# Expert token lists written by indirect transfers in place of one-hot products

## Chip, cores and metric

The kernel runs on one core of one Trainium2 chip. The metric is the device time of one launch in microseconds. Lower is better.

## What is computed

A sequence of 2048 tokens plus 16 meta tokens (2064 in all), 1024 wide, goes through one layer: a pooling mixer, then a mixture of 16 experts in which each expert chooses its tokens, then a last normalisation. The part that matters here, cut from the reference:

```python
cap = CAPACITY_FACTOR * T // N_EXPERTS           # 258
aff = jax.nn.softmax(u @ router_w, axis=-1)
g, idx = lax.top_k(jnp.swapaxes(aff, 1, 2), cap) # per expert: gate and token of each slot
xs = u[idx]                                      # 258 rows of 1024
hid = silu(xs @ w_gate) * (xs @ w_up)            # 2048 wide
ys = (hid @ w_down) * g[..., None]
out = zeros.at[idx].add(ys)
```

A "list" below is the 258 token numbers and gates of one expert.

## The kernel before

**Stages.** The pooling mixer runs over 19 overlapping tiles of 128 tokens (NT = 19). Then comes the routing: affinities, a threshold search over 10 rounds that finds each expert's 258th value, and prefix sums (TensorE) from which `find_slots` works out for each of the 19 x 128 token places and each expert the slot that the token takes in the expert's list, or a slot far off if it isn't chosen. Then a loop over 15 experts (`Fori(0, NE - 1)` on every engine), and expert 15 by itself with the last normalisation beside it.

**One expert.** Products are in fp32 made of two rounded parts: `w_hi` (ScalarE, line 734), `w_lo` (VectorE, line 1061, `split_rest`), and three products for each pair of blocks (`products`, line 1167), 258 columns wide. The work is cut into 48 "quarters" of 24 matmuls, QE = 48: 32 for gate and up (four rounds b of eight, `gate_up`), 16 for down (`down_quarter`). Weights arrive on SP's queue in pieces of 1 MiB into four buffers (`raw`), two quarters a piece, and the splits run up to three quarters ahead of TensorE. `silu` on ScalarE, `hid` and `hid_lo` on VectorE (lines 1090, 1096) stand between the up quarters and the down ones.

**The list of the next expert.** It is made inside the loop for expert n + 1 while expert n runs. On VectorE, after quarter 3 of each round, `pick(n + 1, 5 * b)` compares `iota` with the slot of five token tiles: five one-hot tiles `picks` of 128 x 272 (line 1038), 20 in four rounds. On TensorE, between the last up quarter and the first down quarter, `make_list(n + 1, n + 1)` multiplies the 19 one-hot tiles with `vals` (token number in two digits, affinity in three bf16 parts), 3 x 19 = 57 matmuls. On VectorE, after the split in down quarter 0 and the three copies of the old list (`idx_now`, `gates_now`, `idx_small`, lines 1115 to 1117), `read_list(n + 1)` turns the sums into `idx`, `idx_chunk` and `gates` in six small steps (lines 1044 to 1056). GpSimd waits for them, then starts the three gathers of rows of `u_rows` (`gather`, lines 532, 535), and after the expert's end three accumulating scatters into `h_acc` (lines 578, 580). TensorE turns the gathered rows after down quarter 7 (`turn_pair`).

**Order.** Each engine runs its own list of instructions in order, and semaphores tie them. `carrier` (line 527) is a small GpSimd step ahead of each group of transfers, which carries the waits. `route_v` with `link` chains VectorE's steps in the routing. Where the change reaches the start: `vals` is filled by GpSimd for all experts at once (lines 522, 553, 556), and `loaded_c` counts the constant loads (SMALL = 7).

## Time and profile before

| | us |
|---|---|
| Median of 3 runs | 2557.24 (2557.18 to 2558.84) |
| The profiled execution, its own time | 2560.52 |
| Its span | 2558.7 |
| TensorE busy | 2464.8 (96%) |
| VectorE busy | 1385.4 (54%) |
| ScalarE busy | 1211.9 (47%) |
| GpSimd busy | 195.0 (8%) |

The span is the time between the first and the last instruction in the trace; the run's own time has 1.8 us more around it. Busy times are shares of that span; a matmul row in the trace is longer than its place in the pipeline, so the distance between the starts of two matmuls is what one costs. The chain that ended last is followed back from the last instruction, at each step to what released it.

### The profile page before, as it was taken

To read this page: it belongs to the slowest core of one execution; us is meant where nothing else is said; L and a number is where in the kernel's file an instruction comes from. 1 tells how busy PE (TensorE), PEld (TensorE's weight loads), DVE (VectorE), ACT (ScalarE), POOL (GpSimd) and SP (SyncE) were. 2 spreads that over 40 slices of the span, in tenths; PEclk is the share of its full clock that TensorE was granted. 3 is DMA by queue.
4 is the path that set the end of the run, shared out by engine and by line. 5 is a ranking of instruction groups with operands and counts; after the bars stand their busy time and mean duration, and the time that the engine had idled before them with its cause. 6 is when DMAs were issued, how large, how long until landed. Compare 5 with 4: busy or idle time off the path is not lost.

```text
span 2558.7 us, 55795 instructions
## 1 busy us (share of the span) xinstructions
PE 2464.8 (96%) x21165; PEld 2453.0 (96%) x21165; DVE 1385.4 (54%) x2096; ACT 1211.9 (47%) x1798; POOL 195.0 (8%) x195
## 2 busy tenths in 40 slices
PE   7974999999999999999999999999999999999996
PEld 7964999999999999999999999999999999999996
DVE  5646545555464545555464545555464545555474
ACT  5653444444444444444444444444444444444464
POOL 0020001010101001010101001010101001010101
PEclk9976999999999999999999999999999999999998
DMA  7641566666656566566556566566656566566794
GB/s 218 198 154 50 182 196 190 194 188 199 180 183 195 181 196 189 194 189 199 180 182 195 182 196 188 194 189 200 180 181 196 181 196 187 195 188 201 221 315 171
DMA packets 426301, 485.80 MB, mean 190 GB/s; under 512 B 11537, under 2 KB 406529, under 8 KB 426274
## 3 DMA queue, kind: packets, MB, share of 16 engines
q1 hardware_dynamic: 411106, 433.80, 53.2%
q0 software_dynamic: 10560, 34.87, 5.4%
q10 hardware_dynamic: 4608, 16.78, 1.7%
q8 instruction: 17, 0.28, 0.0%
q14 instruction: 10, 0.08, 0.0%
HBM read 443.21 MB, written 42.21 MB: 190 GB/s over the span
## 4 chain that ended last, share of the span: by engine, by line
PE 96%; DVE 2%; DMA 0%; issue 0%; ACT 0%; POOL 0%; SPq 0%; DVEq 0%; POOLq 0%; ACTq 0%
PE bank L1167 92%; PE bank L1172 3%; DVE marks_v L960 0%; DMA nmix<-in_norm_mix 0%; DMA x_left<-u_rows,idx_chunk 0%; ACT u_t L673 0%; DVE picks L1038 0%; DVE pooled_lo L868 0%; DVE pw L895 0%; DVE key_t L984 0%; DVE y_rows L1159 0%; ACT junk L796 0%; ACT squares L643 0%; ACT pooled_hi L656 0%; DVE flag L967 0%
## 5 line engine op out<-in xcount | busy, mean ns | idle before, releaser
L1061 DVE TENSOR_TENSOR w_lo<-raw,w_hi 128x1024 fp32r<-128x1024 f32 x765 | 930.1, 1222 | 520.7 <-ACT w_hi L734 519.5
L1167 PE MATMUL bank<-x_hi,w_hi 128*128 128x258 f32 x4096 | 1160.8, 283 | 5.6 <-issue 3.7
L1167 PE MATMUL bank<-x_lo,w_hi 128*128 128x258 f32 x4096 | 1163.4, 284 | 0.0
L1167 PE MATMUL bank<-x_hi,w_lo 128*128 128x258 f32 x4096 | 1145.8, 280 | 0.0
L734 ACT ACTIVATE w_hi<-raw 128x1024 fp32r<-128x1024 f32 x765 | 805.0, 1052 | 273.2 <-PE bank L1167 232.1
L1167 PEld LDWEIGHTS bank<-x_hi,w_hi 128*128 128x128 f32 x4096 | 777.9, 190 | 10.1 <-issue 10.1
L1167 PEld LDWEIGHTS bank<-x_hi,w_lo 128*128 128x128 f32 x4096 | 782.6, 191 | 0.0
L1167 PEld LDWEIGHTS bank<-x_lo,w_hi 128*128 128x128 f32 x4096 | 777.4, 190 | 0.0
L1167 PE MATMUL bank<-hid_hi,w_hi 128*128 128x258 f32 x2048 | 586.4, 286 | 0.0
L1167 PE MATMUL bank<-hid_lo,w_hi 128*128 128x258 f32 x2048 | 580.5, 283 | 0.0
L1167 PE MATMUL bank<-hid_hi,w_lo 128*128 128x258 f32 x2048 | 573.8, 280 | 0.0
L1167 PEld LDWEIGHTS bank<-hid_hi,w_lo 128*128 128x128 f32 x2048 | 390.4, 191 | 0.0
L1167 PEld LDWEIGHTS bank<-hid_hi,w_hi 128*128 128x128 f32 x2048 | 388.3, 190 | 0.5
L1167 PEld LDWEIGHTS bank<-hid_lo,w_hi 128*128 128x128 f32 x2048 | 388.3, 190 | 0.0
L1090 DVE TENSOR_TENSOR hid<-silu,bank 128x258 f32<-128x258 f32 x256 | 108.4, 423 | 494.8 <-PE bank L1167 494.8
L785 ACT ACTIVATE hid_hi<-hid 128x258 f32 (+1 forms) x256 | 107.9, 421 | 455.8 <-DVE hid L1090 455.8
L781 ACT ACTIVATE silu<-bank 128x258 f32<-128x258 f32 x256 | 98.7, 385 | 282.3 <-PE bank L1167 282.3
L527 POOL TENSOR_TENSOR carrier<-carrier 128x1 f32<-128x1 f32 x30 | 5.7, 191 | 1994.6 <-DVE gates L1056 1333.7
L809 ACT ACTIVATE y_t<-bank 128x258 f32<-128x258 f32 x128 | 49.3, 386 | 199.4 <-PE bank L1167 199.4
L1096 DVE TENSOR_TENSOR hid_lo<-hid,hid_hi 128x258 f32 (+1 forms) x256 | 108.0, 422 | 0.0
L1038 DVE TENSOR_SCALAR picks<-iota,slot 128x272 bf16 (+1 forms) x320 | 81.7, 288 | 9.3 <-issue 0.4
L578 POOL DMA_INDIRECT h_acc<-y_rows,idx_now x30 | 74.7, 2489 | 12.5 <-issue 12.5
(155 smaller groups left out, 1218.4 us busy)
## 6 DMA issues: line engine op xcount, KB each, us to landing
raw<-in_moe_w_gate SPq DMA_DIRECT2D x128, 1024.0 KB, 5.2
raw<-in_moe_w_up SPq DMA_DIRECT2D x128, 1024.0 KB, 5.2
raw<-in_moe_w_down SPq DMA_DIRECT2D x128, 1024.0 KB, 4.9
h_in<-in_x SPq DMA_DIRECT2D x18, 512.0 KB, 5.6
x_rows<-h_acc ACTq DMA_DIRECT2D x16, 512.0 KB, 5.3
out<-x_rows ACTq DMA_DIRECT2D x16, 512.0 KB, 4.4
h_acc<-h_mid SPq DMA_DIRECT2D x17, 448.0 KB, 4.9
u_rows<-u_out SPq DMA_DIRECT2D x17, 448.0 KB, 3.0
```

Source lines behind the costliest of these rows:

```text
L527: nc.gpsimd.tensor_tensor(carrier[:, 0:1], carrier[:, 1:2], carrier[:, 1:2], ALU.mult)\
L578: pool.indirect_dma_start(h_acc, bass.IndirectOffsetOnAxis(ap=idx_now[:, b:b + 1], axis=0), y_rows[:, b, :], None, compute_op=ALU.add).the ...
L734: nc.scalar.activation(w_hi[:, a % 4], quarter_view(piece % 4, a % 2), ACT.Copy)\
L781: nc.scalar.activation(silu[:, fc], bank[:, q % 4, 0:CAP], ACT.Silu)\
L785: nc.scalar.activation(hid_hi[:, ds(4 * b + fc, 1)], hid[:, fc % 2:fc % 2 + 1], ACT.Copy).then_inc(hid_hi_done, 1)
L809: nc.scalar.activation(y_t[:, m], bank[:, m % 4, 0:CAP], ACT.Copy).then_inc(y_t_done, 1)
L1038: nc.vector.tensor_scalar(picks[:, ds(c0 + c, 1), :], iota[:].unsqueeze(1), src, None, ALU.is_equal).then_inc(picks_done, 1)
L1061: nc.vector.tensor_tensor(w_lo[:, a % 4], quarter_view(a // 2 % 4, a % 2), w_hi[:, a % 4].bitcast(f32), ALU.subtract).then_inc(split_lo, 1)
L1090: nc.vector.tensor_tensor(hid[:, fc % 2], silu[:, fc], bank[:, q % 4, 0:CAP], ALU.mult).then_inc(hid_done, 1)
L1096: nc.vector.tensor_tensor(hid_lo[:, col], hid[:, fc % 2:fc % 2 + 1], hid_hi[:, col].bitcast(f32), ALU.subtract)\
L1167: return nc.tensor.matmul(dst, lhs, rhs, start=start, stop=stop)
L1172: return nc.tensor.matmul(dst, src, ident[0:n, 0:n], is_transpose=True, start=True, stop=True)
```

## The change

The list of expert 0 is made as before. For experts 1 to 15 the one-hot tiles and the 57 products go. Instead:

- `find_slots(1, NE)` writes whole-number slots `slot_rows`; a token that isn't chosen gets slot 4096 + its partition. GpSimd keeps the affinities of all experts in `aff_kept`.
- In the expert loop GpSimd runs `send_list(n)` for expert n + 1: two small copies, then for each of the 19 token tiles one indirect transfer that stores 128 pairs (token number, affinity), 8 bytes each, at row slot of `list_rows` in HBM; slots from 258 on are out of bounds and not stored. Transfer c waits until TensorE has finished c + 2 quarters of expert n, and has a `carrier` step ahead of it. When all have landed, three plain transfers on GpSimd's queue read the list back into `listed_rows` (128 x 2 pairs, and the two left-over rows to 8 partitions each).
- VectorE's `read_list` waits for these reads in the place where it waited for the products, and takes three steps in place of six.
- The start has one more small constant load (`far`), and fills `vals` for expert 0 alone.

```diff
--- before.py
+++ after.py
...
+FAR = 4096
...
@@ -116,6 +117,8 @@
     put("tok_hi", tok // 16)
     put("chunk", k // LEFT)
     put("tok_lo", tok % 16)
+    put("tok", tok)
+    put("far", FAR + k)
...
+    list_rows = nc.dram_tensor("list_rows", [CAP, 2], i32, kind="Internal").ap()
...
-        slot = sb("slot", [P, NE, 20], f32)
-        vals = sb("vals", [P, NE, 20, 5], bf16)
+        slot = sb("slot", [P, 20], f32)
+        vals = sb("vals", [P, 20, 5], bf16)
+        slot_rows = sb("slot_rows", [P, NE, NT], i32)
+        aff_kept = sb("aff_kept", [P, NE, NT], f32)
+        slot_now = sb("slot_now", [P, NT], i32)
+        pair_now = sb("pair_now", [P, NT, 2], i32)
+        listed_rows = sb("listed_rows", [P, 3, 2], i32)
+        far = sb("far", [P, 1], f32)
         listed = sb("listed", [P, 3, 5], f32)
...
-        SMALL = 7
+        SMALL = 8
         XT = KD // 2 + 1
-        LV = 6
+        READS = 3
+        CARRIES = NT + 3
...
             with nc.allow_non_contiguous_dma(reason="a column"):
                 sp.dma_start(chunk[:], consts[:, cols["chunk"][0]:cols["chunk"][1]]).then_inc(loaded_c, 16)
+            with nc.allow_non_contiguous_dma(reason="a column"):
+                sp.dma_start(far[:], consts[:, cols["far"][0]:cols["far"][1]]).then_inc(loaded_c, 16)
             sp.dma_start(reset[:], consts[:, cols["reset"][0]:cols["reset"][1]]).then_inc(loaded_c, 16)
             sp.dma_start(cst[:, POOL_COLS:], consts[:, POOL_COLS:]).then_inc(loaded_c, 16)
             sp.dma_start(nfin[:], norm_final.partition_broadcast(P)).then_inc(loaded_c, 16)
...
             for k, name in enumerate(("tok_hi", "tok_lo")):
-                nc.gpsimd.tensor_copy(vals[:, 0:NE, 0:NT, k],
-                                      const(name).unsqueeze(1).broadcast_to([P, NE, NT])).then_inc(vals_done, 1)
+                nc.gpsimd.tensor_copy(vals[:, 0:NT, k], const(name)).then_inc(vals_done, 1)
+            nc.gpsimd.tensor_copy(pair_now[:, :, 0], const("tok")).then_inc(list_copied, 1)
...
-            src = aff[:, 0:NT, :]
+            src = aff[:, 0:NT, 0]
             pool.wait_ge(bits_split, 2)
             for c0 in range(0, NT, 4):
                 c1 = min(c0 + 4, NT)
                 nc.gpsimd.tensor_copy(key[:, 1, c0:c1], many_keys(1, c0, c1)).then_inc(keyed_p, 1)
+            nc.gpsimd.tensor_copy(aff_kept[:].rearrange("p e c -> p c e"), aff[:, 0:NT, :]).then_inc(aff_saved, 1)
             for k in range(3):
-                dst = vals[:, 0:NE, 0:NT, 2 + k].rearrange("p e c -> p c e")
+                dst = vals[:, 0:NT, 2 + k]
                 nc.gpsimd.tensor_copy(dst, src).then_inc(vals_done, 1)
...
+            def send_list(n):
+
+                pool.wait_ge(list_copied, 2 * n + 1)
+                nc.gpsimd.tensor_copy(slot_now[:], slot_rows[:, ds(n + 1, 1), :].rearrange("p a c -> p (a c)"))\
+                  .then_inc(list_copied, 1)
+                nc.gpsimd.tensor_copy(pair_now[:, :, 1].bitcast(f32),
+                                      aff_kept[:, ds(n + 1, 1), :].rearrange("p a c -> p (a c)"))\
+                  .then_inc(list_copied, 1)
+                pool.wait_ge(list_copied, 2 * n + 3)
+                for c in range(NT):
+                    pool.wait_ge(quarters, QE * n + c + 2)
+                    pool.wait_ge(carrier_set, CARRIES * n + 1 + c)
+                    carry_wait()
+                    pool.indirect_dma_start(list_rows, bass.IndirectOffsetOnAxis(ap=slot_now[:, c:c + 1], axis=0),
+                                            pair_now[:, c, :], None, bounds_check=CAP - 1, oob_is_err=False)\
+                        .then_inc(list_sent, 16)
+                pool.wait_ge(list_sent, 16 * NT * n + 16 * NT)
+                pool.wait_ge(carrier_set, CARRIES * n + 1 + NT)
+                carry_wait()
+                with nc.allow_non_contiguous_dma(reason="a list of pairs"):
+                    pool.dma_start(listed_rows[:, 0:2, :], list_rows[0:256, :].rearrange("(b p) v -> p b v", p=P))\
+                        .then_inc(list_read, 16)
+                    for t in range(LEFT):
+                        pool.dma_start(listed_rows[t:SMALL_ROWS:LEFT, 2, :],
+                                       list_rows[256 + t].partition_broadcast(KD)).then_inc(list_read, 16)
+
...
-            pool.wait_ge(list_v, LV)
+            pool.wait_ge(list_ready, 3)
             gather()
+            pool.wait_ge(slotted, 1)
+            pool.wait_ge(aff_saved, 1)
             with pool.Fori(0, NE - 1) as n:
-                pool.wait_ge(list_v, LV * n + 2 * LV)
-                pool.wait_ge(carrier_set, 2 * n + 1)
+                send_list(n)
+                pool.wait_ge(list_ready, 3 * n + 6)
+                pool.wait_ge(carrier_set, CARRIES * n + 2 + NT)
                 pool.wait_ge(x_turned, XT * n + XT)
                 carry_wait()
                 gather()
                 pool.wait_ge(y_rows_done, 5 * n + 5)
                 pool.wait_ge(list_kept, 3 * n + 3)
-                pool.wait_ge(carrier_set, 2 * n + 2)
+                pool.wait_ge(carrier_set, CARRIES * n + 3 + NT)
                 pool.wait_ge(scattered, 48 * n)
                 carry_wait()
                 for b in range(2):
...
-                link(nc.vector.scalar_tensor_tensor(out=place[:, es], in0=place[:, es], scalar=-NEG_SLOT - SLOT0,
-                                                    in1=chosen[:, es], op0=ALU.add, op1=ALU.mult))
-                link(nc.vector.tensor_scalar(slot[:, es, 0:NT], place[:, es], NEG_SLOT, None, ALU.add))
+                if e0 == 0:
+                    link(nc.vector.scalar_tensor_tensor(out=place[:, es], in0=place[:, es],
+                                                        scalar=-NEG_SLOT - SLOT0, in1=chosen[:, es],
+                                                        op0=ALU.add, op1=ALU.mult))
+                    link(nc.vector.tensor_scalar(slot[:, 0:NT], place[:, 0], NEG_SLOT, None, ALU.add))
+                else:
+                    link(nc.vector.scalar_tensor_tensor(out=place[:, es], in0=place[:, es], scalar=far[:, 0:1],
+                                                        in1=chosen[:, es], op0=ALU.subtract, op1=ALU.mult))
+                    nc.vector.tensor_scalar(slot_rows[:, es], place[:, es], far[:, 0:1], None, ALU.add)\
+                      .then_inc(slotted, 1)
 
             dve.wait_ge(prefixed, 4)
             find_slots(0, 1)
 
...
-            def read_list(m):
-
-                dve.wait_ge(listed_ps, m + 1)
+            def read_first_list():
+
+                dve.wait_ge(listed_ps, 1)
                 nc.vector.tensor_copy(listed[:, 0:2], bank[:, 6, 0:10].rearrange("p (b v) -> p b v", v=5))\
                   .then_inc(list_v, 1)
                 nc.vector.tensor_copy(listed[0:SMALL_ROWS, 2], bank[0:SMALL_ROWS, 6, 10:15]).then_inc(list_v, 1)
-                dve.wait_ge(list_v, LV * m + 2)
+                dve.wait_ge(list_v, 2)
                 nc.vector.tensor_tensor(part[:], listed[:, :, 4], listed[:, :, 3], ALU.add).then_inc(list_v, 1)
-                dve.wait_ge(gathered, 48 * m)
                 nc.vector.scalar_tensor_tensor(out=idx[:], in0=listed[:, :, 0], scalar=16.0,
                                                in1=listed[:, :, 1], op0=ALU.mult, op1=ALU.add)\
-                  .then_inc(list_v, 1)
-                dve.wait_ge(list_v, LV * m + 4)
+                  .then_inc(list_ready, 1)
+                dve.wait_ge(list_ready, 1)
                 nc.vector.scalar_tensor_tensor(out=idx_chunk[:], in0=idx[:, 2:3], scalar=float(KD),
-                                               in1=chunk[:], op0=ALU.mult, op1=ALU.add).then_inc(list_v, 1)
-                nc.vector.tensor_tensor(gates[:], part[:], listed[:, :, 2], ALU.add).then_inc(list_v, 1)
+                                               in1=chunk[:], op0=ALU.mult, op1=ALU.add).then_inc(list_ready, 1)
+                dve.wait_ge(list_v, 3)
+                nc.vector.tensor_tensor(gates[:], part[:], listed[:, :, 2], ALU.add).then_inc(list_ready, 1)
+
+            def read_list(m):
+
+                dve.wait_ge(list_kept, 3 * m)
+                dve.wait_ge(list_read, 16 * READS * m)
+                dve.wait_ge(gathered, 48 * m)
+                nc.vector.tensor_copy(idx[:], listed_rows[:, :, 0]).then_inc(list_ready, 1)
+                nc.vector.scalar_tensor_tensor(out=idx_chunk[:], in0=listed_rows[:, 2, 0:1], scalar=float(KD),
+                                               in1=chunk[:], op0=ALU.mult, op1=ALU.add).then_inc(list_ready, 1)
+                nc.vector.tensor_copy(gates[:], listed_rows[:, :, 1].bitcast(f32)).then_inc(list_ready, 1)
...
-                    if q == 3 and not last:
-                        dve.wait_ge(listed_ps, n + 1)
-                        pick(n + 1, 5 * b)
...
@@ -1111,7 +1176,7 @@
 
                         dve.wait_ge(scattered, 48 * n)
                         dve.wait_ge(y_rows_done, 5 * n)
-                        dve.wait_ge(list_v, LV * n + LV)
+                        dve.wait_ge(list_ready, 3 * n + 3)
                         nc.vector.tensor_copy(idx_now[:], idx[:]).then_inc(list_kept, 1)
...
-            def make_list(e, m):
-
-                first = isinstance(m, int)
-                if not first:
-                    pe.wait_ge(picks_done, 20 * m + 20)
-                    pe.wait_ge(y_rows_done, 5 * m - 5)
+            def make_first_list():
+
                 for b, (s0, n) in enumerate(TOK_BLOCKS):
                     if b == 2:
                         n = SMALL_ROWS
                     for c in range(NT):
-                        if first and b == 0 and c % 5 == 0:
+                        if b == 0 and c % 5 == 0:
                             pe.wait_ge(picks_done, c + 5)
-                        v = vals[:, ds(e, 1), c, :].rearrange("p a v -> p (a v)")
-                        last = mm(bank[0:n, 6, 5 * b:5 * b + 5], picks[:, c, s0:s0 + n], v, c == 0, c == NT - 1)
+                        last = mm(bank[0:n, 6, 5 * b:5 * b + 5], picks[:, c, s0:s0 + n], vals[:, c, :],
+                                  c == 0, c == NT - 1)
                 last.then_inc(listed_ps, 1)
...
-                if i == 2:
-                    pe.wait_ge(list_v, LV * m + 2)
+                if i == 2 and isinstance(m, int):
+                    pe.wait_ge(list_v, 2)
...
                 with pe.Fori(0, 4) as b:
                     gate_up(n, b)
-                make_list(n + 1, n + 1)
                 for q in range(16):
                     down_quarter(n, q)
```

## Rows read from the trace of the kernel before

**Rows 1.** The page's busy times: engine, busy us, share, instructions.

```profile
PE 2464.8 (96%) x21165; PEld 2453.0 (96%) x21165; DVE 1385.4 (54%) x2096; ACT 1211.9 (47%) x1798; POOL 195.0 (8%) x195
```

**Rows 2.** Chain that ended last, whole span: start us, us, what.

```profile
526.34 116.93 PE bank L1167 x1017
...
644.14 2.87 PE bank L1167 x24
...
2253.90 116.95 PE bank L1167 x1017
```

**Rows 3.** Waits of thirteen experts: engine, line, releaser, total us, times, longest.

```profile
ACT w_hi L734 <- PE bank L1167: 186.5, 100, 2.8
...
PE bank L1167 <- issue: 3.5, 13, 0.3
```

**Rows 4.** One expert: busy us of PE, PEld, DVE, ACT, POOL; PEclk, DMA share, GB/s.

```profile
395.00:540.00 145.00, 144.73 (x1254) 144.28 (x1253) 78.24 (x117) 68.47 (x100) 10.10 (x8) 1.00 0.61 190
```

**Rows 5.** Timeline of TensorE around one list: start, us, engine, line, operation.

```profile
618.08 0.28 PE L1167 MATMUL bank<-x_hi,w_lo 128*128 128x258 f32 x1
...
618.20 1.93 PE L1167 MATMUL bank<-vals,picks 128*128 x57
620.06 0.39 PE L1167 MATMUL bank<-hid_hi,w_hi 128*128 128x258 f32 x1
620.28 0.28 PE L1167 MATMUL bank<-hid_lo,w_hi 128*128 128x258 f32 x1
```

**Rows 6.** Timeline of VectorE over the same stretch.

```profile
608.83 1.44 DVE L1038 TENSOR_SCALAR picks<-iota,slot 128x272 bf16 x5
610.18 2.36 DVE L1061 TENSOR_TENSOR w_lo<-raw,w_hi 128x1024 fp32r<-128x1024 f32 x2
...
618.82 1.22 DVE L1061 TENSOR_TENSOR w_lo<-raw,w_hi 128x1024 fp32r<-128x1024 f32 x1
619.96 0.42 DVE L1096 TENSOR_TENSOR hid_lo<-hid,hid_hi 128x258 f32 x1
620.46 1.22 DVE L1061 TENSOR_TENSOR w_lo<-raw,w_hi 128x1024 fp32r<-128x1024 f32 x1
```

**Rows 7.** Lines 621, 578, 1061: count, ns min/median/max, landing.

```profile
L621 POOL DMA_INDIRECT out<-y_rows,idx_out x3: 890/980/1168, 2544.8 to 2547.6; - x3
...
DMA to landing us min/median/max: 2.6/3.5/3.5
...
L578 POOL DMA_INDIRECT h_acc<-y_rows,idx_now x30: 1852/2507/2667, 384.4 to 2402.9; - x30
...
L1061 DVE TENSOR_TENSOR w_lo<-raw,w_hi x765: 1215/1223/1228, 235.7 to 2528.9; 128x1024 fp32r<-128x1024 f32 x192
```

**Rows 8.** Timeline of GpSimd over one expert, idle before in brackets.

```profile
528.36 2.66 POOL L578 DMA_INDIRECT h_acc<-y_rows,idx_now  x1 [0.53 <-issue]
...
534.00 1.33 POOL L580 DMA_INDIRECT h_acc<-y_small,idx_small  x1 [0.30 <-issue]
622.85 0.19 POOL L527 TENSOR_TENSOR carrier<-carrier 128x1 f32<-128x1 f32 x1 [87.51 <-DVE gates L1056]
```

**Rows 9.** DMA issues: size and median us to landing.

```profile
raw<-in_moe_w_gate SPq DMA_DIRECT2D x128, 1024.0 KB, 5.2
```

**Rows 10.** Timeline of the start.

```profile
12.75 0.43 SPq L438 DMA_DIRECT2D chunk<-in_consts  x1
...
21.05 0.29 POOL L518 CAST tri_b<-cst 128x128 bf16<-128x128 f32 x1 [17.96 <-DMA nfin<-in_norm_final]
...
22.87 0.16 DVE L852 RECIPROCAL inv<-rms 128x1 f32<-128x1 f32 x1 [3.81 <-ACT rms L631]
```

**Rows 11.** Timeline of VectorE in the threshold search.

```profile
183.26 0.69 DVE L958 TENSOR_TENSOR ahead<-cand,cst 128x1 f32<-128x1 f32 x1 [2.20 <-ACT key_t L705]
...
186.14 0.53 DVE L958 TENSOR_TENSOR ahead<-cand,cst 128x1 f32<-128x1 f32 x1
...
188.71 0.16 DVE L958 TENSOR_TENSOR ahead<-cand,cst 128x1 f32<-128x1 f32 x1
```

35 lines of the change are left out of this document (21 added, 14 removed).

## Prediction, made before the changed kernel was built or timed

> **What bounds the kernel now.** I read the page's busy times first: TensorE is busy 96% of the span [rows 1]. A pipelined matmul row makes TensorE look busier than it is, so I went on to the chain of waits, which says whether anything but TensorE ends last. It does not, in the expert loop: each expert is one long piece of products, a few turns and another piece, and the same instruction comes back every (2253.90 - 526.34) / 12 = 143.96 us [rows 2]. The long piece has 1017 matmuls: 32 gate and up quarters of 24, the list of 57, and 8 down quarters of 24. One quarter of 24 takes 2.87 us [rows 2], 0.12 us a matmul. The waits view of thirteen experts gives TensorE only 0.3 us a time of idle, from no other engine, and ScalarE's weight rounding waits for TensorE, never for a weight load [rows 3]. Granted clock is 1.00, and the DMA engines are busy 0.61 of the time, VectorE 78 of 145 us, GpSimd 10 [rows 4]. So a matmul that leaves TensorE in this loop is worth its place there, unless what it hid comes out.
>
> **What the list costs TensorE.** The 57 list matmuls sit between the last up quarter and the first down quarter. The last up product starts at 618.08, the first list product at 618.20, the first down product at 620.06 and the second at 620.28 [rows 5]. With no list, the first down product would start 0.12 us after the last up product, at 618.20, and the second at 618.32. The list therefore holds 620.06 - 618.20 = 1.86 us, and 1.96 us if the slow first step after it (0.22 in place of 0.12) goes too. I take 1.96: within one kind of product the steps are 0.12. There are 15 such lists: 15 x 1.86 = 27.9 us at least, 15 x 1.96 = 29.4 us taken. The list of expert 0 stays.
>
> **What the list hid.** This is the step on which the forecast stands. Down quarter 0 would start at 618.20, quarters 1 to 3 at 621.07, 623.94 and 626.81, quarter 4 at 629.7. Their low weight halves are the w_lo splits on VectorE: those for quarter 0 end at 610.18 + 2.36 = 612.5, quarter 1 before the next row shown, at 618.8 at the latest, quarter 2 at 620.0, quarter 3 at 621.7 [rows 6]. Quarter 2 also wants the last hid_lo, which ends at 620.4. The least slack is 2.3 us by that bound for quarter 1, and 3.5 us for quarter 2, so nothing there comes out. The splits for quarters 2 and 3 follow the last hid product, whose start hangs on the end of the last up quarter and not on the list, so they stay where they are. Had a cover been missing, its cost would be at most the 1.96 us, per expert.
>
> **VectorE's part.** Twenty picks per expert (five take 1.44 us, so 5.8 us an expert [rows 6]) and six reading steps become three. Its 78 of 145 us fall to about 72. It gives nothing to the end, as VectorE waits for others already.
>
> **GpSimd's part, the new work.** Per expert: two small copies, 19 indirect transfers, each behind a wait on a quarter, a wait for all of them, three plain reads of the list, and a carrier step before each group. The trace has no transfer of 8-byte pairs. Nearest row below: the indirect store to out, 128 rows with a bounds check, 890 to 1168 ns on GpSimd, landing 3.5 us; nearest above: the accumulating scatter, up to 2667 ns [rows 7]. With the carrier step (0.19), the start gap after it (0.53) and the gap after a transfer (0.30) [rows 8], one send costs 0.98 + 1.02 = 2.0 us, at most 2.67 + 1.02 = 3.7. I take 2.0, since the store to out has the same number of rows and the same check. Against quarters of 2.87 us the sends then run at the quarters' pace: 19 x 2.0 = 38 us of work spread to quarter 20, 526.34 + 20 x 2.87 = 583.7. A landing (3.5) and three reads (2.0 each, again a landing) end it by 583.7 + 2.0 + 3.5 + 6.0 + 3.5 = 599.
>
> What waits behind it: the list is read by VectorE after the copies of idx that follow down quarter 0's split, at 620.46 + 1.22 = 621.7 [rows 6], so there are 22 us over. Queued behind this reading on VectorE is the split for down quarter 4, needed at 629.7, and behind that on TensorE everything. On GpSimd, the gather of the next expert stands behind the sends; it starts at 622.9 now [rows 8] and is needed for the turns after down quarter 7, at 641. Behind the gather is the scatter, which waits for the end of the expert anyway. The sends themselves stand behind the scatter of the expert before, which ends on GpSimd at 534.00 + 1.33 = 535.3 [rows 8].
>
> **The Trainium skill against this change.** The traced weight loads land in 5.2 us at 1 MiB, and the small store lands in 3.5 us for far fewer bytes [rows 7, 9]: small transfers pay a nearly fixed time. The Trainium skill, "DMA: Bandwidth & Descriptors", Rules for kernel authors, says to coalesce small transfers, which pay mostly overhead, and its Anatomy section gives about 2.0 us fixed for each. By that, an estimate of 19 x 2.0 = 38 us an expert even if nothing overlapped, which would leave the sum as it is.
>
> **Weight loads.** A piece is released by the split of the quarter seven before the one whose split needs it, so it has 7 x 2.87 = 20 us to land in, and lands in 5.2 [rows 9]. The pairs add 19 x 128 x 8 bytes, 19 KB, at most, to 24 pieces of 1 MiB of weights. I cost it at nothing; loads would have to slow down about four times before TensorE saw it.
>
> **The start.** The added load: one more load of a column goes on SP's queue, like chunk's, 0.43 us of issue [rows 10], and delays the constants behind it (reset, cst, nfin) by that much. VectorE is waiting then for ScalarE's rms until 22.87 while the constants are there at 21.05 [rows 10]: 1.8 us of cover, so nothing. During the threshold search two GpSimd subtractions over 304 columns go; VectorE's step "ahead" takes 0.69 and 0.53 us beside them where it takes 0.16 elsewhere [rows 11]. VectorE's part of the chain could shorten by 0.53 + 0.37 = 0.9 us at most, by nothing at least. I take 0.5, since the smaller subtractions still run in that stretch.
>
> **Sum.** 29.4 + 0.5 = 29.9 us. The profiled execution took 2560.5 us around its span of 2558.7, and would come to 2530.6; the median, 2557.2, is 3.3 us lower, and goes to 2527.3. By the lower bounds (27.9 and 0) it is 2529.3.
>
> **The rivals.**
> (a) The list's time is given back. The place of the list turns into a wait of the first down quarters, or of the turns after quarter 7 for the gather, or the matmuls were in truth covered. It gives 2557, no change; a half gives 2542. For it: the loop is tight, five engines meet there. Against: slacks of 2.3 us and more [rows 6], and a gather that starts 18 us before its turn.
> (b) The list comes late, slower than before. From the end of the scatter, 535.3, to the last moment at which VectorE may go on to the split of quarter 4 (629.7 - 1.2 = 628.5, less 0.4 of reading) there are 92.8 us. Less the last landing, the reads and theirs (13), 80 us stay for 19 sends: 4.2 us each. From that point each microsecond a send costs 19 us an expert and 285 us in all. At 5 us a send, 0.8 over, the kernel takes 2527 + 228 = 2755. For it: 19 transfers in a row on one queue are in no stretch of this trace, and the largest row (2.67) gives 3.7, not far off. Against: every row with 128 plain rows is under half of the 4.2.
> (c) GpSimd is kept from its work by VectorE. A scatter at 528.36 takes 2.66 us beside a split, others 1.85 [rows 7, 8]; if each send also waited out one 1.22 us split, 2.0 + 1.2 = 3.2 us would still fit, but 3.7 + 1.2 = 4.9 would not, and 0.7 x 285 = 200 us gives 2727. In the other direction, the splits never exceed 1228 ns in 765 [rows 7], so VectorE isn't held up by transfers. The Trainium skill, "SBUF — State Buffer", Who interferes with whom, has GpSimd and VectorE share a port pair as an exclusive lock, the loser blocked for the whole instruction. The trace agrees as far as the two "ahead" steps go.
> (d) The pairs cost the DMA engines far more than their bytes, and the weight stream lags by part of its cover: a few us to some tens, say 2535 to 2555.
>
> **How the numbers follow.** Forecast, the full gain: 0.80, 2525 to 2531. (a) 0.08, half of it with part of the gain left. (b) 0.05. (c) 0.03. (d) 0.04. The likeliest is 2527.5. The range, 2525 to 2535, holds the forecast case with both bounds and 2 us of scatter between runs, and the near end of (a) and (d): about 0.82. About 0.2%, 5 us, is what a measurement of this kernel can tell from none. Faster by more than that: 0.80, with half of (a) and most of (d), 0.87. Within it: the rest of those, 0.05. Slower: (b) and (c), 0.08.
>
> **What would show it.** After: the long piece with 960 matmuls in place of 1017 and some 115.0 us; a period of 142.0 us; no list products but the first 57; no idle of TensorE from VectorE. GpSimd's sends spaced at 2.87 us with 1.0 us each, some 45 us busy per expert less what hides in gaps, and the gather still starting within 3 us after the first split of the down part. Wrong would be: sends closer than the pace because they are behind it, VectorE idle before copying idx, TensorE idle before down quarters 0 to 4, weight loads landing in over 20 us.

## The result and the profile after

The changed kernel takes 2524.66 us (median of 4 runs, 2524.11 to 2527.45) against 2557.44 (4 runs, 2557.18 to 2558.84) for the kernel before: 32.8 us less, a ratio of 0.9871, 95% interval 0.9856 to 0.9887. The kernel is faster, as forecast, but the gain is 2.9 us more than the sum's 29.9, and the time lies 0.34 us under the range of 2525 to 2535. Its profiled execution took 2524.75 us, with a span of 2522.9. Of the kernels below, three had one execution each far above its others (4830.61, 6156.38 and 3045.49 us), and their medians are those of the fast executions.

The page's busy times after, to be read against [rows 1]:

```profile
PE 2432.7 (96%) x20310; PEld 2423.2 (96%) x20310; DVE 1317.0 (52%) x1751; ACT 1212.2 (48%) x1798; POOL 686.6 (27%) x858
```

TensorE has 855 matmuls less, 15 lists of 57. VectorE is busy 68 us less, GpSimd 492 us more. Of the chain of work that ended last (start us, us, what):

```profile
233.92 116.47 PE bank L1232 x960
...
519.35 114.94 PE bank L1232 x960
...
2222.59 114.94 PE bank L1232 x960
2364.29 120.83 PE bank L1232 x1008
...
2486.43 17.22 PE bank L1232 x144
```

The long piece went from 1017 matmuls in 116.93 us [rows 2] to 960 in 114.94, and the period, which is the time of one expert, from 143.96 to (2222.59 - 519.35) / 12 = 141.94 us: 2.02 us an expert, 30.3 for the 15 lists. The waits of experts 2 to 13 (engine, line, releaser, us in all, times, longest) and one period by windows (us, then the busy time of PE, PEld, DVE, ACT and POOL, granted clock, DMA share, GB/s):

```profile
POOL carrier L548 <- DMA list_rows<-pair_now,slot_now: 29.9, 13, 2.8
ACT w_hi L785 <- PE bank L1232: 160.8, 99, 2.0
...
PE bank L1232 <- issue: 3.1, 13, 0.2
```

```profile
519.35:661.29 141.94, 141.70 (x1186) 141.42 (x1187) 72.78 (x92) 67.43 (x99) 42.48 (x52) 1.00 0.64 192
```

TensorE still waits for no engine and no transfer; its one row is the 0.2 us a turn that [rows 3] has too. The clock is 1.00, VectorE is down from 78 us of 145 to 73 of 142, GpSimd up from 10 to 42. Where the list was [rows 5], TensorE's timeline now reads:

```profile
611.07 0.28 PE L1232 MATMUL bank<-x_hi,w_lo 128*128 128x258 f32 x1
611.19 0.28 PE L1232 MATMUL bank<-hid_hi,w_hi 128*128 128x258 f32 x1
611.31 0.28 PE L1232 MATMUL bank<-hid_lo,w_hi 128*128 128x258 f32 x1
```

The first down product follows the last up product by 0.12 us, and the second by another 0.12. Both halves of the forecast 1.96 us are gone. VectorE at the same place (compare [rows 6]):

```profile
613.46 1.23 DVE L1129 TENSOR_TENSOR w_lo<-raw,w_hi 128x1024 fp32r<-128x1024 f32 x1
...
615.08 0.17 DVE L1121 COPY idx<-listed_rows 128x3 int32<-128x3 int32 x1 [0.19 <-DVE idx_small L1182]
...
615.35 1.22 DVE L1129 TENSOR_TENSOR w_lo<-raw,w_hi 128x1024 fp32r<-128x1024 f32 x1
```

Line 1121 is the reader of the new list, and the instruction that the rival "the list comes late" hangs on. It waits 0.19 us, for its own engine and for no transfer. GpSimd's sends and the gather behind them (to set against [rows 8]):

```profile
537.00 0.18 POOL L548 TENSOR_TENSOR carrier<-carrier 128x1 f32<-128x1 f32 x1 [1.08 <-PE bank L1232]
537.70 0.99 POOL L595 DMA_INDIRECT list_rows<-pair_now,slot_now  x1 [0.52 <-issue]
539.86 0.18 POOL L548 TENSOR_TENSOR carrier<-carrier 128x1 f32<-128x1 f32 x1 [1.18 <-PE bank L1232]
540.56 1.67 POOL L595 DMA_INDIRECT list_rows<-pair_now,slot_now  x1 [0.52 <-issue]
542.73 0.18 POOL L548 TENSOR_TENSOR carrier<-carrier 128x1 f32<-128x1 f32 x1 [0.49 <-PE bank L1232]
543.43 1.67 POOL L595 DMA_INDIRECT list_rows<-pair_now,slot_now  x1 [0.52 <-issue]
545.60 0.74 POOL L548 TENSOR_TENSOR carrier<-carrier 128x1 f32<-128x1 f32 x1 [0.49 <-PE bank L1232]
...
616.79 1.06 POOL L553 DMA_INDIRECT x_rows<-u_rows,idx  x1 [0.16 <-issue]
```

The sends follow each other by 2.86 and 2.87 us, a quarter's pace, each released by TensorE. The send that takes 1.67 us and the carrier step that takes 0.74 run into a split on VectorE:

```profile
540.15 1.22 DVE L1129 TENSOR_TENSOR w_lo<-raw,w_hi 128x1024 fp32r<-128x1024 f32 x1
...
545.06 1.23 DVE L1129 TENSOR_TENSOR w_lo<-raw,w_hi 128x1024 fp32r<-128x1024 f32 x1 [0.48 <-ACT w_hi L785]
```

All of them, and the reads of the list with their landings (from issue, min/median/max):

```profile
L595 POOL DMA_INDIRECT list_rows<-pair_now,slot_now x285: 976/1055/2018, 242.4 to 2281.1; - x143
...
L602 POOL DMA_DIRECT2D listed_rows<-list_rows x15: 775/786/809, 298.5 to 2286.0; - x15
...
DMA to landing us min/median/max: 3.0/3.2/3.5
```

In the threshold search both slow "ahead" steps of [rows 11] are gone:

```profile
182.02 0.16 DVE L1009 TENSOR_TENSOR ahead<-cand,cst 128x1 f32<-128x1 f32 x1 [1.98 <-ACT key_t L756]
...
184.64 0.16 DVE L1009 TENSOR_TENSOR ahead<-cand,cst 128x1 f32<-128x1 f32 x1
```

**The end.** What no part of the prediction looked at: the last step of each chain, and the span. First the kernel before, then the changed one.

```profile
core 0 of [0], span 2558.7 us
...
2547.57 0.89 POOL out L621
```

```profile
core 0 of [0], span 2522.9 us
...
2514.47 0.89 POOL out L672
```

From the start of the last transfer to the end it is 11.13 us before and 8.43 after, with the same transfer (two rows), which lands in 2.6 us in both. Here are 2.70 of the 35.8 us between the two spans. The trace's instruction records, which hold more than the views of busy work, show what fills it: DRAIN, the last instruction but two of GpSimd, starts 0.2 us behind the last landing and takes 8.16 us before and 5.50 after.

**The rest of the 35.8 us.** The two profiled executions also differ in TensorE's granted clock before the loop is well under way. First the kernel before, then the changed one (windows, columns as above):

```profile
150.00:160.00 10.00, 8.79 (x51) 8.59 (x51) 2.69 (x4) 2.36 (x4) 0.00 (x0) 0.67 0.89 314
```

```profile
150.00:160.00 10.00, 8.22 (x58) 7.91 (x57) 3.81 (x5) 2.83 (x5) 0.00 (x0) 0.83 0.89 306
```

The clock has two levels here, 1.00 (2.4 GHz) and 0.50 (1.2 GHz), and such a value is the mean of a stretch. From 236 to 260 us it is 0.88 before and 0.94 after, and the first long piece, 119.71 us before and 116.47 after, shortens by 1.2 us more than the later ones do. It also begins 1.7 us earlier (235.63 and 233.92), of which 0.8 lies at the two "ahead" steps. So the 35.8 us are 30.3 in the loop, 1.2 in the first long piece, 1.7 ahead of it and 2.7 at the end, less 0.2 for the last expert's products, which take 120.83 us instead of 120.58: 35.7.

### The profile page after: what moved, and what is told of

The parts are those of the page before. It is cut to its first block, busy times and chain, and to the rows that moved or that the text cites. A ratio compares the mean times of both kernels' runs of the same rounds, so it can differ in the third digit from the quotient of the medians.

```text
span 2522.9 us, 54344 instructions
## 1 busy us (share of the span) xinstructions
PE 2432.7 (96%) x20310; PEld 2423.2 (96%) x20310; DVE 1317.0 (52%) x1751; ACT 1212.2 (48%) x1798; POOL 686.6 (27%) x858
## 4 chain that ended last, share of the span: by engine, by line
PE 96%; DVE 2%; DMA 1%; ACT 0%; issue 0%; POOL 0%; SPq 0%; DVEq 0%; ACTq 0%; POOLq 0%
PE bank L1232 93%; PE bank L1237 3%; DVE marks_v L1011 0%; DMA nmix<-in_norm_mix 0%; DMA x_left<-u_rows,idx_chunk 0%; ACT u_t L724 0%; DVE picks L1095 0%; DVE pooled_lo L919 0%; DVE pw L946 0%; DVE key_t L1035 0%; DVE y_rows L1224 0%; ACT junk L847 0%; ACT squares L694 0%; ACT pooled_hi L707 0%; DVE flag L1018 0%
## 5 line engine op out<-in xcount | busy, mean ns | idle before, releaser
L548 POOL TENSOR_TENSOR carrier<-carrier 128x1 f32<-128x1 f32 x330 | 118.6, 359 | 1338.3 <-ACT y_small L883 632.8
L595 POOL DMA_INDIRECT list_rows<-pair_now,slot_now x285 | 378.1, 1327 | 127.8 <-issue 124.5
L629 POOL DMA_INDIRECT h_acc<-y_rows,idx_now x30 | 55.9, 1864 | 12.5 <-issue 12.5
```

The source lines that it names most:

```text
L548: nc.gpsimd.tensor_tensor(carrier[:, 0:1], carrier[:, 1:2], carrier[:, 1:2], ALU.mult)\
L595: pool.indirect_dma_start(list_rows, bass.IndirectOffsetOnAxis(ap=slot_now[:, c:c + 1], axis=0), pair_now[:, c, :], None, bounds_check=CAP ...
L629: pool.indirect_dma_start(h_acc, bass.IndirectOffsetOnAxis(ap=idx_now[:, b:b + 1], axis=0), y_rows[:, b, :], None, compute_op=ALU.add).the ...
```

## The experiments

Seven kernels test the steps of the prediction, the nine others the end. "Tail" is the time from the start of the last transfer to the end of the span.

**No sends** (e1_no_send). The lists are neither sent nor read; the indices of expert 0's list serve all.

```
-                send_list(n)
-                nc.vector.tensor_copy(idx[:], listed_rows[:, :, 0]).then_inc(list_ready, 1)
+                nc.vector.tensor_copy(idx[:], idx_now[:]).then_inc(list_ready, 1)
```

> The changed kernel with no sends and no reads of the list: experts 1 to 15 work again on the list of expert 0, so their output is left out of the comparison. Theory A (the new work of GpSimd and of the DMA queue costs nothing, the gain is the place of the 57 products on TensorE): the time of the changed kernel, 2524.7 us, within 1 us, and the same period of 141.94 us an expert. Theory B (sends cost something that a larger gain hides): faster by 3 us or more, 2521.5 or less.

2528.27 us, ratio 0.9879 (0.9864 to 0.9894): 3.6 us slower than with the sends, where theory A had it within 1 us. The chain:

```profile
516.43 114.95 PE bank L1230 x960
...
2219.89 114.94 PE bank L1230 x960
...
2488.14 17.22 PE bank L1230 x144
```

The period is (2219.89 - 516.43) / 12 = 141.95 us, with the sends 141.94. So 285 sends and 45 reads cost TensorE nothing: theory A holds for the loop and misses outside it. The profiled execution is 4.4 us longer than the changed kernel's, the sum of three differences. The tail is 11.11 us, as before the change and 2.7 more than after it, and the DRAIN is back at 8.16 us: the sends and reads together had shortened it. The last expert's last run of products starts (2488.14 - 2219.89) - (2486.43 - 2222.59) = 4.4 us later behind the last long piece of the loop; the chain there goes through a store of 7.1 us, ScalarE and a split that TensorE waits for. Against these, that piece itself starts 2.7 us earlier. Expert 15 sends nothing, so the 4.4 us aren't time spent on sends; why the last stage falls so isn't shown.

**List products kept** (e2_products_kept). The changed kernel with the 57 products of each list back in their place, their result unused.

```
+                    for c in range(NT):
+                        mm(bank[0:k_, 6, 5 * b:5 * b + 5], picks[:, c, s0:s0 + k_], vals[:, c, :],
+                            c == 0, c == NT - 1)
```

> The changed kernel with the 57 list products put back on TensorE for experts 1 to 15, on the old tiles of expert 0; their result is not used; no picks and no reading of the sums. Theory A (all of the loop's gain is the products' place, 1.96 to 2.02 us each): 2524.7 + 15 x 2.0 = 2554.7 us, period 143.9. Theory C (part of the gain comes from the picks that left VectorE or from other waits): less comes back, under 2550.

2552.82 us, ratio 0.9976 (0.9965 to 0.9987), 28.2 us above the changed kernel.

```profile
379.89 116.73 PE bank L1232 x1017
...
2248.21 116.73 PE bank L1232 x1017
```

```profile
615.50 1.67 PE L1232 MATMUL bank<-vals,picks 128*128 128x5 bf16 x57
617.10 0.39 PE L1232 MATMUL bank<-hid_hi,w_hi 128*128 128x258 f32 x1
```

The long piece is 1.79 us longer than 114.94, and 15 x 1.79 = 26.9 of the 28.2 us; the period is (2248.21 - 379.89) / 13 = 143.72 us. Theory A holds. So the gain is the place of the products on TensorE, and the sends bring nothing by themselves. The tail stays at 8.46 us: the products have no part in it. The list takes 1.60 us from first product to first down product here and 1.86 in [rows 5]. The kernel before read its operands at an address taken from a register (the expert's number), this one at a fixed address; 0.26 us over 57 matmuls goes with that, though no run isolates it. Nor do the periods: the kernel before with three reads once, further down, keeps its list products as they were and has 143.84 us, so 0.12 of the 0.24 us between 143.96 and 143.72 come and go with the products' form unchanged.

**The old start** (e3_old_start). The three roundings and two subtractions over all experts are back on GpSimd during the threshold search.

```
+                dst = vals_all[:, 0:NE, 0:NT, 2 + k].rearrange("p e c -> p c e")
+                nc.gpsimd.tensor_copy(dst, src_all).then_inc(all_done, 1)
+                    nc.gpsimd.tensor_tensor(rest_all[:], src_all, dst, ALU.subtract).then_inc(all_done, 1)
```

> The changed kernel with GpSimd's old conversions of the affinities of all 16 experts put back beside the new ones in the threshold search (3 casts and 2 subtractions over 304 columns, 6.7 us of GpSimd, result unused). Theory D (these held up VectorE at the start of the search): two slow steps named ahead come back, and 0.5 to 0.9 us with them: 2525.5 us; Theory E (the start's gain is the moment at which the clock changes, by chance): the slow steps may come back but the time stays within the scatter of 2524.1 to 2527.5, and the clock of the stretch 150 to 160 us differs between profiles whatever the kernel.

2524.55 us, ratio 0.9867 (0.9852 to 0.9882), no different from the changed kernel. VectorE and GpSimd in the search:

```profile
181.80 0.16 DVE L1021 TENSOR_TENSOR ahead<-cand,cst 128x1 f32<-128x1 f32 x1 [2.20 <-ACT key_t L768]
182.07 1.01 POOL L582 TENSOR_TENSOR rest_all<-aff,vals_all 128x304 f32<-128x304 f32 x1
...
184.43 0.16 DVE L1021 TENSOR_TENSOR ahead<-cand,cst 128x1 f32<-128x1 f32 x1
184.79 0.98 POOL L582 TENSOR_TENSOR rest_all<-rest_all,vals_all 128x304 f32<-128x304 f32 x1
```

The long subtractions are back, but each begins 0.27 and 0.36 us after "ahead" has begun, when "ahead" is over, and it keeps its 0.16 us. In [rows 11] it had 0.69 and 0.53, with the subtraction begun first. So theory D falls: the cost is that the two meet in time, which the subtractions' presence doesn't settle. It was 0.9 us in the first profile of the kernel before and 1.2 in its repeat, and it is missing in the kernel before with three reads once, whose subtractions are the old ones.

**The kernel before, once more** (e4_before_again), to see what repeats.

> The kernel before, unchanged, timed against itself. The ratio is 1.000. Theory E (the 1.3 us in the stretch 148 to 156 us, the 1.2 us in expert 0's first round and the 2.7 us after the last transfer are moments of the clock and of the end that differ from one execution to the next): this second profile has other values there than the first one, nearer to those of the changed kernel: a first long piece of 116.5 + 3 = near 118.5 us in place of 119.71, or a tail under 22 us. Theory F (the change itself moved them): the second profile repeats 119.71 and 21.95 within 0.2 us.

2558.3 us, ratio 1.0005 (0.9996 to 1.0014). Its first long piece takes 118.48 us where the first profile has 119.71 (the changed kernel: 116.47, and 117.52 with the old start), and begins 0.83 us earlier. The slow "ahead" steps are there again (0.89, 0.66 us), and so is the tail: 11.18 us, with a DRAIN of 8.16. So theory E is right for the first piece and the start, which move by about a microsecond between executions of one kernel, and theory F for the tail, which doesn't.

**Sends later by 10 and by 14 quarters** (e7_late12, e8_late16), and **not paced at all** (e11_unpaced).

```
-                    pool.wait_ge(quarters, QE * n + c + 2)
+                    pool.wait_ge(quarters, QE * n + c + 12)
```

(16 in place of 12 in the second; in the third this line is left out.)

> Each send waits for ten quarters more (c + 12 in place of c + 2), so that the last is released by quarter 30. By the profile of the changed kernel the list is there 10.3 us, 3.6 quarters, after the quarter that releases the last send: at quarter 33.6, where VectorE asks for it at 32.5 and holds the split that TensorE needs at 36. Theory A (the list has a deadline at 35.4 quarters, before which lateness is free): the time of the changed kernel, 2524.7 us within 2 us. Theory J (any wait of VectorE for the list costs its length): 1.1 quarters, 3.2 us an expert, 2572 us.

2523.96 us, ratio 0.9866 (0.9849 to 0.9882); the period stays at 141.94 us. The reader of the list now waits for it, 1.0 us a turn, and it costs nothing, so theory J falls:

```profile
DVE idx L1121 <- DMA listed_rows<-list_rows: 12.3, 12, 1.2
```

> Each send waits for fourteen quarters more (c + 16), the last released by quarter 34. The list is there at quarter 37.6, VectorE reads it and makes the split of down quarter 4 by 38.15, which TensorE wants at 36.0. Theory A: 2.15 quarters, 6.2 us an expert, 93 us in all: 2618 us. Theory K (the splits of the next quarters queue up behind, so more is lost): over 2650 us. That the rival of a late list has its price where the prediction put it is what the two runs tell together.

2606.56 us, ratio 1.0185 (1.0165 to 1.0206), 81.9 us above the changed kernel. The waits:

```profile
DVE idx L1121 <- DMA listed_rows<-list_rows: 117.3, 12, 10.1
PE bank L1232 <- DVE w_lo L1129: 40.1, 12, 3.7
```

The list is 9.8 us late, and of those 3.3 reach TensorE: the rest is slack in front of the split of down quarter 4, as the prediction's deadline says. But one period, from 2006.03 to 2153.33, is 5.36 us longer, 2.0 more than the mean wait. The product that ends the idle time in that turn, and a window table over it (columns as above):

```profile
2113.04 0.39 PE L1232 MATMUL bank<-hid_hi,w_hi 128*128 128x258 f32 x1 [3.55 <-DVE w_lo L1129]
```

```profile
2110.00:2113.00 3.00, 0.00 (x0) 0.00 (x0) 1.45 (x5) 0.86 (x1) 1.35 (x2) 1.00 0.04 1
2113.00:2115.00 2.00, 1.96 (x12) 1.96 (x13) 2.00 (x2) 0.00 (x0) 1.84 (x2) 0.76 0.00 0
2115.00:2118.00 3.00, 3.00 (x18) 3.00 (x17) 1.39 (x2) 0.26 (x1) 2.39 (x3) 0.59 0.91 293
2118.00:2122.00 4.00, 4.00 (x36) 4.00 (x35) 1.53 (x2) 1.86 (x2) 0.38 (x1) 1.00 1.06 381
```

After TensorE's idle time of 3.5 us the granted clock averages 0.76 and then 0.59, between its two levels, and is back at 1.00 by 2118: 18 matmuls in 3 us instead of 25. The four quarters behind the idle time take 13.3 us instead of 11.5. So the rival's mechanism is real, and its price is the wait and, in most turns, about 1.8 us of clock. Theory K, over 2650 us, falls. The 93 us of theory A came near for another reason than its own: it had 6.2 us of lateness a turn and no clock, the run 3.3 us of wait and the clock.

> The changed kernel without the waits on the quarters: the 19 sends run one behind the other right after the scatters. Theory A: the pace buys nothing on TensorE; 2524.7 us within 1.5 us, sends 2.2 us apart. Theory N (sends that come close together hold up weight loads or VectorE): slower by 3 us or more.

2526.78 us, ratio 0.9877 (0.9857 to 0.9897), which can't be told from the changed kernel (scatter 3.3 us), though it is 2.1 above where theory A allowed 1.5; theory N had 3 or more. Sends without the wait:

```profile
530.12 2.00 POOL L594 DMA_INDIRECT list_rows<-pair_now,slot_now  x1 [0.16 <-issue]
...
535.24 0.99 POOL L594 DMA_INDIRECT list_rows<-pair_now,slot_now  x1 [0.15 <-issue]
...
536.62 0.99 POOL L594 DMA_INDIRECT list_rows<-pair_now,slot_now  x1 [0.16 <-issue]
```

The nineteen of this expert start at 528.66 to 560.92 us, 1.79 us apart in the mean, 1.38 at the least (the last two shown) and 3.0 at the most. The 2.0 us of the prediction is near the mean and above it, as the gaps are smaller here than it took, and sends at that rate don't hurt the weight loads either (period 141.94).

**What sets the end.** First the two halves of the sending by themselves: sends without reads of the list (e5_sends_only), and reads of other rows without sends (e6_reads_only). Both go on with expert 0's list.

> The changed kernel with its 19 indirect sends an expert, but without the three reads back; experts 1 to 15 work on the list of expert 0, so their output is left out of the comparison. One look, for the stretch between the start of the last transfer to out and the end of the span: 11.1 us in the two profiles of the kernel before and with no sends, 8.4 us in the changed one. Theory G (the indirect sends shorten it): 8.4 us. Theory H (the plain reads on GpSimd's queue shorten it): 11.1 us. Period of an expert 141.94 us by both.

> The changed kernel without the 19 sends, but with three plain reads of the same shapes an expert on GpSimd's queue, from u_rows, into the same tile, result unused; experts 1 to 15 work on the list of expert 0, so their output is left out. One look at the same stretch. Theory G: 11.1 us. Theory H: 8.4 us.

2522.82 and 2517.65 us, with tails of 9.9 and 5.08. Neither half alone gives the changed kernel's 8.43, so neither G nor H holds. Then the kernel before with more code and with more transfers (48 small memsets on GpSimd; 45 plain reads of 8-byte pairs on its queue during the pooling stage):

> The kernel before with 48 tiny memsets more on GpSimd at the start, where GpSimd waits for constants anyway; no transfer added. One look at the stretch from the start of the last transfer to out to the end of the span. Theory L (it depends on what GpSimd's queue has been given before): 11.1 us as in the kernel before. Theory M (it depends on the length and place of GpSimd's code): some other value, off by over 0.5 us.

> The kernel before with 45 small plain reads more on GpSimd's queue during the pooling stage (15 times three, of the shapes of the list reads), result unused. One look at the same stretch. Theory L: 5.1 us, as in the kernel with reads only, which had put the same 141 transfers and 12000 packets on the queue; the span falls by 6 us. Theory M: near 11.1, or any value that goes with the code and not with 5.1.

2560.02 and 2554.72 us (one execution each, as for the two above); the tails are 11.11 and 11.07, unchanged. Neither more code nor the number of transfers in the program alone sets it. In the next five kernels the same reads stand elsewhere on GpSimd's queue; in the first of them this group is in the expert loop:

```
+                with nc.allow_non_contiguous_dma(reason="pairs"):
+                    pool.dma_start(spare[:, 0:2, :], x2[0:256, 0:2].rearrange("(b p) v -> p b v", p=P)).then_inc(spare_read, 16)
+                    for t in range(LEFT):
+                        pool.dma_start(spare[t:SMALL_ROWS:LEFT, 2, :], x2[256 + t, 0:2].partition_broadcast(KD)).then_inc(spare_read, 16)
```

> The kernel before with three plain reads of 8-byte pairs on GpSimd's queue in every turn of the expert loop (45 in all, the count that the kernel with 45 reads ahead of the loop had), nothing else changed; its output is the reference's. What stays open is the end of the program: the instruction that fills it in the trace is GpSimd's closing DRAIN, 8.16 us in the kernel before, in its repeat, with 48 more memsets and with 45 plain reads ahead of the loop; 6.93 with the sends alone; 5.50 in the changed kernel; 2.16 with the reads alone in the expert loop. Theory K (it goes by what stands on GpSimd's queue within the expert loop, whatever the rest of the kernel is): the DRAIN takes 2.2 us here, the tail 5.1 us. Theory M (it goes by something else in the changed kernel, its tensors, its buffers or its code): 8.2 us and 11.1 as before. The rest of the time as before: 2557 us with M, 2551 with K.

> The kernel before with three plain reads of 8-byte pairs on GpSimd's queue once, between the last expert's row gathers and the final stage; its output is the reference's. Theory N (the DRAIN goes by how lately GpSimd issued a plain transfer, one is enough): 2.2 us, tail 5.1. Theory O (it goes by the number of them, or by their place in a loop among the gathers): 8.2 us and tail 11.1, or a value between for three of 45 (7.8).

> The changed kernel with the same three plain reads once between the last expert's row gathers and the final stage; its output is the reference's. Theory N: the DRAIN falls from 5.50 us to 2.2 and the time to 2521.4 us, under both kernels. Theory O: 5.5 us, tail 8.4, 2524.7. If it goes by a position that every transfer moves on, another value than either.

> The kernel before with 21 plain reads of 8-byte pairs once (seven groups of three, each group behind the landing of the one before) between the last expert's row gathers and the final stage; its output is the reference's. Three of them lengthened GpSimd's closing DRAIN by 0.245 us in both kernels, and 45 in the expert loop shortened it by 6.00 us. Theory P (the DRAIN goes by a position that every transfer moves on and that returns to its start: 45 reads are 15 x 0.245 = 3.68 us on, less one turn, so a turn is 3.68 + 6.00 = 9.68 us): 8.156 + 7 x 0.245 = 9.87 is past the turn, the DRAIN takes 0.2 us and the tail 3.1. Theory Q (it only adds up): 9.87 us, tail 12.8. The DRAIN is what is read here; the final stage itself may start some us later behind the reads.

> The changed kernel with 54 plain reads of 8-byte pairs in all: a group of three in every turn of the expert loop (45) ahead of the send of the rows, and three groups once behind the loop; its output is the reference's. Theory P: 5.503 + 18 x 0.245 = 9.91 us is past the turn of 9.68, so the DRAIN takes 0.23 us, the tail 3.2 us, and the time is 5.3 us under the changed kernel's: 2519.4 us, faster than both. Theory Q: 9.9 us, tail 12.8, 2529.1.

In order, they took 2549.92, 2555.3, 2524.76 (ratio 0.9868, 0.9852 to 0.9884), 2572.97 and 2529.08 us (ratio 0.9886, 0.9869 to 0.9902); the first, second and fourth are single executions. In the fourth the reads hold up GpSimd's work for the final stage, as expected, and the last is 4.4 us above the changed kernel, of which the DRAIN is 1.7. Theory K's time for the reads in the loop holds: a DRAIN of 2.153 us, within 2 ns of that with the reads alone. Its rule, that only the loop counts, doesn't, since three reads behind the loop add 0.245 us in either kernel. Theory N falls with them. P and Q both fall: 6.20 and 7.22 us, where P had 0.2 and 0.2, Q 9.9 and 9.9. All together, from the records:

```
kernel                                        transfers on     DRAIN   tail
                                              GpSimd's queue   us      us
before, again, more code, no sends            99               8.16    11.1
before + 3 reads once                         102              8.40    11.4
before + 21 reads once                        120              6.20    9.2
before + 45 reads ahead of the loop           144              8.15    11.1
before + 45 reads in the loop                 144              2.15    5.1
reads only                                    144              2.16    5.1
sends only                                    384              6.93    9.9
changed; products kept; old start; late;
  unpaced                                     429              5.50    8.4 to 8.5
changed + 3 reads once                        432              5.75    8.8
changed + 54 reads (45 in the loop)           483              7.22    10.3
```

Three transfers more are 0.245 us, 0.0817 each, and 99 x 0.0817 = 8.09 us is nearly the whole DRAIN of the kernel before. Some of the other differences come out in whole steps of that size: from 99 to 120 transfers 1.96 us off, 24 steps; from 99 to 384, 1.22 off, 15; from 429 to 483, 1.715 more, 21. But the kernel before and the changed one lie 2.65 us or 32.5 steps apart, and the 45 reads in the loop take off 6.00 us, 73.5 steps. A tally of transfers that GpSimd works off at 0.082 us each, most of it on the way and the rest in the DRAIN, would explain the whole steps and not the half ones, so it stays a guess. The records show the length of the DRAIN and not what it does. What decides its length stays open: not the count alone (144 gives 8.15 or 2.15 by the place of the reads).

## Where the prediction held, and the step that failed

- **What bounds the kernel**: right. TensorE's products in a row set the period in every version but the one with sends 14 quarters later, and no other engine or transfer stands in TensorE's waits after the change.
- **The list's place, 1.86 to 1.96 us**: the right mechanism, a little small. It measured 2.02 an expert by the period, 30.3 us instead of 29.4. The products kept in their place account for 1.79 of it. The other 0.23 goes in part with the form that they had in the kernel before; how it divides isn't shown.
- **What the list hid: nothing**: right. The first two down products come at 0.12 us steps, and the slack was there.
- **VectorE's part, nothing**: right; 78 us of 145 went to 73 of 142, with no effect on the end.
- **GpSimd's part**: near for one send (2.0 us with its carrier step and gaps; unpaced sends come 1.79 apart in the mean, 1.38 to 3.0 in one expert), and right in that there is a deadline far behind. Paced, a send takes 0.98 us at least and 1.06 at the median. Begun while a split of VectorE runs, one takes 1.67 us, and a carrier step 0.74 in place of 0.18. The trace agrees here with the rule cited from the Trainium skill, "SBUF — State Buffer", Who interferes with whom: GpSimd's step, begun second, loses 0.6 to 0.7 us, the carrier step until the split ends, and the pace of 2.87 us swallows it.
- **Against "coalesce small transfers"**: a read of 2 KB of the list lands in 3.0 to 3.5 us and its small reads of 8 pairs in 2.3 to 3.0, where a weight piece of 1 MiB lands in 5.2 [rows 9]. (The prediction's own pair of rows was a weak one: its "small store" of 128 rows is 512 KiB, half a weight piece.) That small transfers pay mostly overhead is what the Trainium skill, "DMA: Bandwidth & Descriptors", Rules for kernel authors, says, and the trace agrees. But the price is a latency: with 19 sends under way behind each other, GpSimd waits for a landing once an expert, 29.9 us in 13 times, 2.3 each, far from the end.
- **Weight loads, nothing**: right, at a DMA share of 0.64 instead of 0.61.
- **The start**: 0.5 us was taken. Both slow "ahead" steps are gone, which would give 0.9, but the old work put back doesn't bring them back. Whether the steps meet hangs on when each starts, and a figure for it was a guess between two bounds.
- **The end of the program**: the step that failed. It has no term in the sum: "It would come to 2530.6" took everything outside the loop and the search over unchanged, without a reason. But GpSimd's queue went from 99 transfers to 429, and the closing DRAIN from 8.16 us to 5.50; with sends and reads taken out it is 8.16 again. These 2.7 us are nearly all of the 2.9 by which the gain passed the forecast: 30.3 + 2.7 - 0.2 (the last expert's products) = 32.8 us, as by the medians. Without them the time would have been 2527.3 us, where the likeliest was put at 2527.5. So close a match has luck in it: the sum has nothing for the start, and the four executions of the changed kernel lie 3.3 us apart. The 0.34 us by which the time leaves the range are far below that scatter; the missing 2.7 us are there in every profile. For the profiled execution alone the sum is 35.7 of 35.8 us, as worked out above, with some 2 us, ahead of the second expert, that lie mostly in stretches at different granted clocks.
- **The range**: its low end stood 2.5 us under the forecast, for scatter alone. A gain outside the loop had no room. The same range with 2.7 us more on that side would have held the time.
- **Rivals**: (a) no time was given back. (b) is real and lay between 10 and 14 quarters off: free at 10 quarters later, 81.9 us at 14. Its price left out the clock, which adds about 1.8 us to each 3.3 us wait. (c) and (d) show as longer steps on GpSimd and a higher DMA share, and cost nothing.

## What to carry to other kernels

When one engine runs without a gap, taking work from it is worth its place there. Some 30 us a period of small transfers on an idle engine and queue were free here, paced or not, because they were ready before their reader. Find the reader's deadline by the wait that stands in front of the bound engine, and test it by sending later on purpose. A sum for the whole program needs a term for what lies behind the last landing whenever the change adds transfers to GpSimd's queue: read the stretch from the start of the last transfer to the end of the span in the trace before (11.1 us here, 5.1 to 11.4 in the variants), and widen the range for it. And whether short steps on two engines meet hangs on when each starts: don't count their parting as a gain of the edit.

## What the runs showed of the hardware

- GpSimd's closing DRAIN took between 2.15 and 8.40 us. It was 8.156 us in both profiles of the kernel before and 5.503 in all six kernels with 429 transfers. Three plain reads behind the loop made it 0.245 us longer in either kernel; 45 reads in the loop made it 6.00 shorter, and the kernel before about 8 us faster (one execution).
- After 3.5 us without a product, TensorE's granted clock, 1.00 until then, fell to a mean of 0.76 over 2113 to 2115 us and 0.59 over 2115 to 2118, and was 1.00 again behind that.
- An indirect transfer of 128 pairs of 8 bytes occupies GpSimd for 0.98 us, as a store of 128 rows of 4 KiB does (0.98 [rows 7]), and the store of two such rows for 0.89: neither the size nor the number of rows shows much.
